# Longer fill at nine stage boundaries, and two products of tile 0 set apart in each stage's first block

## The chip, the cores and the metric

The kernel runs on one core of one Trainium2 chip. The metric is device microseconds of one execution; the time before is the median of three runs, 1781.67 us (1781.33 to 1782.0).

## The reference, cut to what matters

Two transformer blocks of width 1024 run on 256 tokens, each with two layers, so that ten sublayers follow each other. Each is a normalised and modulated input, a body, and a gated residual:

```python
h, g = modulate(x, norm_g[i, 0], c_act, mod_w[i, 0], mod_b[i, 0])   # rmsnorm * (1 + scale) + shift
x = x + 0.5 * g * swiglu(h, ffn_w_gate[i, 0], ffn_w_up[i, 0], ffn_w_down[i, 0])
...
y = mamba2_mixer(...)   # or moba_mixer, stick_breaking_attention, dsa_attention, conv_ffn
x = x + g * y
```

The order of the bodies is ffn, mamba, ffn, ffn, moba, ffn, sb, cffn, dsa, cffn. The weights are fp32, some 280 blocks of 128x2048 elements (1 MB) in all.

## The kernel before

**Stages.** One stage of the program is one sublayer; they are numbered 0 to 9. The activations lie transposed in SBUF: `h` has eight tiles (kk = 0 to 7) of 128 features by 256 tokens. Every fp32 product is made of three fp32r products: both operands are split into a high part and a low remainder, and the kernel adds high x high, high x low and low x high (helper `three`, lines 1573 to 1575). ScalarE makes the high parts of the weights (L495), VectorE their low parts (L913), three buffers in rotation; TensorE works through the blocks in the order in which they lie in memory.

**Tile 0 lies apart.** The low part of `h` is two tensors: tiles 1 to 7 in `h_lo_rest`, tile 0 in `h_lo_first`, with an unused tensor of 16 words before it and one of 48 words behind it:

```python
h_hi = sb("h_hi", [P, KT, T], F32R)
h_lo_rest = sb("h_lo_rest", [P, KT - 1, T], F32R)
gap = sb("gap", [P, 16])
h_lo_first = sb("h_lo_first", [P, T], F32R)
gap2 = sb("gap2", [P, 48])
```

So `h_hi` and `h_lo_rest` begin at the same offset modulo 128 bytes, and `h_lo_first` begins 64 bytes off it. In all later blocks of a stage the products with kk = 0 are written in the order low tile, high tile, low weight (lines 1630 to 1632), once for each half of the output.

**A stage boundary.** The last block of a stage (`last`) ends with the sums of squares for the next norm (`summed_squares`, L1686, or `squares`, L1669). TensorE then runs `fill(st + 1)` (L1695): products whose result goes to a bank that nobody reads before it is overwritten; both operands come from the first weight block of the next stage. Meanwhile ScalarE makes the reciprocal root (L499, L501), VectorE the eight scaled tiles (L1034), ScalarE the eight high tiles `h_hi` (L529, semaphore `hhi`), VectorE the eight low tiles (L1041, semaphore `hlo`) and then the last quarter of the second block's low weights (L920).

**The first block of a stage** (`gemm` with `first=True`) has a high part and a low part. The high part waits for `hhi` of each kk and multiplies it with high and low weights for both halves of the output (L1586, L1589: 32 products). The low part waits for `hlo` of each kk and multiplies it with the high weights, (kk, m) in the order (0,0), (0,1), (1,0), (1,1) to (7,0), (7,1) (L1600: 16 products). In stage 0 the high part is ordered a little differently (low weights in a loop of their own, L1595), the low part is the same, and the second block begins with pairs of low tile (L1606) and high tile (L1608). In stages 1 to 9 what follows is the next block, or the small products of mamba or dsa (`three` with `ws_hi`).

Of the kernel before, what the change touches and what calls it, by code (L numbers as in the profile page):

```python
# [30 lines left out]
KT = D // P  # L31
# [9 lines left out]
MAMBA_SIDE = [None] + [("item", q) for q in (29, 30, 31)] + [("fold", (2, part)) for part in range(4)]  # L41
HELD = range(32, 36)
RESCALED = 6
FILL = {0: 0, RESCALED: 28}
AHEAD = 2
NRAW = 6
NW = 3
# [203 lines left out]
def build(nc, weights, mods, params, consts, xin, out, stages=None):  # L251
# [3 lines left out]
    with ExitStack() as ctx:  # L255
# [16 lines left out]
        def h_lo(kk):  # L272

            return h_lo_rest[:, kk - 1, :] if kk else h_lo_first[:, :]
# [1280 lines left out]
        def _(eng):  # L1555
            k = Steps(eng, plan, sems)

            def begin(st, i, a, b):

                if st == 0 and isinstance(i, int) and i == 0 and b == 0:  # L1560
                    eng.wait_ge(sems["half_lo"], 1)
                elif st == 0 and isinstance(i, int) and i == 0 and b == 1:
                    eng.wait_ge(sems["whi"], k.block(0, b=1) + 1)
                elif st and isinstance(i, int) and i == 0 and b == 1:
                    eng.wait_ge(sems["part"], st)
                else:
                    eng.wait_ge(sems["wlo"], k.block(st, i, a, b) + 1)
                s = k.block(st, 0 if a % NW == 0 else i, a, b) % NW
                return [w[s][:, :] for w in (w_hi, w_lo)]

            def three(dst, ah, al, bh, bl, start, stop, skip=False):

                eng.matmul(dst, ah, bh, start=start, stop=False, skip_group_check=skip)  # L1573
                eng.matmul(dst, ah, bl, start=False, stop=False, skip_group_check=skip)  # L1574
                return eng.matmul(dst, al, bh, start=False, stop=stop, skip_group_check=skip)  # L1575

            def gemm(dst, st, i=0, a=0, b=0, tokens=False, first=False, between=None):

                hi, lo = [w.rearrange("p (k n) -> p k n", k=KT) for w in begin(st, i, a, b)]
                both = [(m, slice(m * P, (m + 1) * P), dst[:, m * T:(m + 1) * T]) for m in range(2)]  # L1580
                if first:

                    for kk in range(KT):
                        k.wait("hhi", st, b=kk)
                        for m, part, d in both:
                            eng.matmul(d, hi[:, kk, part], h_hi[:, kk, :], start=kk == m == 0, stop=False,  # L1586
                                       skip_group_check=True)
                            if st:
                                eng.matmul(d, lo[:, kk, part], h_hi[:, kk, :], start=False, stop=False,  # L1589
                                           skip_group_check=True)  # L1590
                    for kk in range(0 if st else KT):
                        if kk == 4:
                            eng.wait_ge(sems["wlo"], 1)
                        for m, part, d in both:
                            eng.matmul(d, lo[:, kk, part], h_hi[:, kk, :], start=False, stop=False,  # L1595
                                       skip_group_check=True)
                    for kk in range(KT):
                        k.wait("hlo", st, b=kk)
                        for m, part, d in both:
                            mm = eng.matmul(d, hi[:, kk, part], h_lo(kk), start=False, stop=kk == KT - 1,  # L1600
                                            skip_group_check=True)
                elif st == 0 and isinstance(i, int) and i == 0 and b == 1:

                    for kk in range(KT):
                        for m, part, d in both:
                            eng.matmul(d, hi[:, kk, part], h_lo(kk), start=kk == m == 0, stop=False,  # L1606
                                       skip_group_check=True)
                            eng.matmul(d, hi[:, kk, part], h_hi[:, kk, :], start=False, stop=False,  # L1608
                                       skip_group_check=True)
                    eng.wait_ge(sems["wlo"], k.block(0, b=1) + 1)  # L1610
                    for kk in range(KT):
                        for m, part, d in both:
                            mm = eng.matmul(d, lo[:, kk, part], h_hi[:, kk, :], start=False, stop=kk == KT - 1,
                                            skip_group_check=True)
                else:
                    for m, part, d in both:
                        if m and between:
                            between()
                        for kk in range(KT):
                            if m == 0 and kk == 6 and st and isinstance(i, int) and i == 0 and b == 1:  # L1620
                                eng.wait_ge(sems["wlo"], k.block(st, b=1) + 1)
                            if tokens and kk == 0:
                                eng.matmul(d, h_lo(kk)[:, part], hi[:, kk, :], start=True, stop=False)
                                eng.matmul(d, h_hi[:, kk, part], hi[:, kk, :], start=False, stop=False)
                                eng.matmul(d, h_hi[:, kk, part], lo[:, kk, :], start=False, stop=False)
                            elif tokens:
                                mm = three(d, h_hi[:, kk, part], h_lo(kk)[:, part], hi[:, kk, :], lo[:, kk, :],
                                           kk == 0, kk == KT - 1)
                            elif kk == 0:
                                eng.matmul(d, hi[:, kk, part], h_lo(kk), start=True, stop=False)  # L1630
                                eng.matmul(d, hi[:, kk, part], h_hi[:, kk, :], start=False, stop=False)  # L1631
                                eng.matmul(d, lo[:, kk, part], h_hi[:, kk, :], start=False, stop=False)  # L1632
                            else:
                                mm = three(d, hi[:, kk, part], lo[:, kk, part], h_hi[:, kk, :], h_lo(kk),
                                           kk == 0, kk == KT - 1)
                mm.then_inc(sems["blk"], 1)
# [53 lines left out]
            def fill(st):  # L1690


                hi = begin(st, 0, 0, 0)[0].rearrange("p (k n) -> p k n", k=KT)
                for n in range(FILL.get(st, 14)):
                    eng.matmul(bank[5][:, 0:T], hi[:, n % KT, 0:P], hi[:, n % KT, :], start=True, stop=True)  # L1695

            def norm(st):
# [7 lines left out]
            def ffn(st):  # L1705
# [3 lines left out]
                def gate(i, a, b, first=False):  # L1709
                    if not first:  # L1710
                        k.wait(free4, st, i, per4, -per4)
                    gemm(bank[4], st, i, a, b, first=first)

                def up(i, a, b, first=False):
                    if not first:
                        k.wait(free5, st, i, per5, -1)
                    gemm(bank[5], st, i, a, b)
# [29 lines left out]
            def last(st, ready, early=0, token_squares=None):  # L1747
# [37 lines left out]
                if more:  # L1785
                    fill(st + 1)

            def mamba(st):
# [73 lines left out]
                def body(i, a, b):  # L1862
                    more = i > 0
                    k.wait("xdt", st, i, 1, -1)
                    gemm(bank[4], st, i, a, b, first=not more)
                    if more:
                        more_rows(i)
                    else:
                        timestep()
                    k.wait("cbs", st, i, 1, -1)  # L1870
                    gemm(bank[5], st, i, a, b + 1, between=None if more else timestep_columns)
                    if more:
                        y_out(i)
                        k.wait("dec", st, i, 4, -1)
                    gemm(bank[7], st, i, a, b + 2)
                    if not more:
                        cum()
                    parts(i)
                    if more:
                        gemm_out(st, i, a, b + 3, lambda kk: k.wait("alo", st, i, 1, -1) if kk == 0 else None, i == 1)  # L1880
                    first_rows(i)
# [354 lines left out]
```

## Time and profile before

| | |
|---|---|
| median of 3 runs | 1781.67 us |
| profiled execution, its own time | 1790.81 us |
| its span | 1789.0 us |
| granted TensorE clock, mean | 0.999 |
| TensorE busy | 1749.9 us (98%), 14686 matmuls |
| VectorE / ScalarE busy | 1452.8 us (81%) / 956.5 us (53%) |
| chain that ended last | TensorE 90%, VectorE 4%, ScalarE 3%, DMA 2% |

TensorE's ends are modelled and its matmuls overlap: one is listed at some 280 ns, but the next starts some 115 ns later. So the distance from start to start, called the pitch below, is what a matmul costs, and not its listed duration.

### The profile page before, as it was taken

Reading aid. Unit: us, or ns where it says so; the run is one execution under the profiler, and the core shown is the slowest. Engines: PE = TensorE matmul, PEld = TensorE weight load, DVE = VectorE, ACT = ScalarE, POOL = GpSimd, SP = SyncE. Lnnn points to the kernel's source line nnn. Section 1 sums busy time; section 2 is a strip of 40 time slices with the busy share of each in tenths; the row PEclk is TensorE's granted clock in tenths of the full one; section 3 lists DMA queues with packets and bytes.
Section 4 is the critical chain, followed back from the end, with each engine's and each line's share of the span. In section 5 each row is a group of like instructions: output and inputs, shape, how many; then the busy total and the mean of one; then the engine's idle time right before and its main releaser. Section 6 shows DMA issues by size and latency. Waiting matters only on the chain.

```text
span 1789.0 us, 34260 instructions
## 1 busy us (share of the span) xinstructions
PE 1749.9 (98%) x14686; PEld 1700.5 (95%) x14686; DVE 1452.8 (81%) x1749; ACT 956.5 (53%) x1254; POOL 0.2 (0%) x4
## 2 busy tenths in 40 slices
PE   5999999999999999999999999999999999999999
PEld 4999999998999999999999999999999998989999
DVE  7799898888898889898557989765899887567766
ACT  4443466665533354445766444565655556775553
POOL 0000000000000000000000000000000000000000
PEclk9999999999999999999999999999999999999999
DMA  9998834344597949895444989343288545415551
GB/s 396 414 419 307 322 141 154 134 173 154 219 410 312 373 167 386 326 393 193 170 152 186 388 329 378 134 163 139 110 304 292 206 147 177 151 73 214 187 197 37
DMA packets 68149, 426.23 MB, mean 238 GB/s; under 512 B 7488, under 2 KB 10832, under 8 KB 31824
## 3 DMA queue, kind: packets, MB, share of 16 engines
q1 hardware_dynamic: 63936, 416.22, 60.5%
q10 hardware_dynamic: 4112, 8.62, 1.4%
q8 instruction: 68, 1.11, 0.2%
q14 instruction: 33, 0.27, 0.0%
HBM read 423.74 MB, written 3.17 MB: 239 GB/s over the span
## 4 chain that ended last, share of the span: by engine, by line
PE 90%; DVE 4%; ACT 3%; DMA 2%; issue 0%; DVEq 0%; SPq 0%; ACTq 0%
PE bank L1573 24%; PE bank L1574 24%; PE bank L1575 24%; PE bank L1630 2%; PE bank L1632 2%; PE bank L1631 2%; DMA raw<-weights 1%; PE bank L1686 1%; PE bank L1989 1%; DMA mix<-mods 1%; PE bank L1586 1%; PE bank L1600 1%; PE bank L1589 1%; PE bank L1822 1%; ACT w_hi L495 1%; DVE work L1034 1%
## 5 line engine op out<-in xcount | busy, mean ns | idle before, releaser
L1573 PE MATMUL bank<-h_hi,w_hi 128*128 128x256 f32 x2504 | 696.0, 278 | 0.0
L1574 PE MATMUL bank<-h_lo_rest,w_hi 128*128 128x256 f32 x2504 | 694.9, 278 | 0.0
L1575 PE MATMUL bank<-h_hi,w_lo 128*128 128x256 f32 x2504 | 694.8, 277 | 0.0
L913 DVE TENSOR_TENSOR w_lo<-raw,w_hi 128x2048 fp32r<-128x2048 f32 x267 | 609.5, 2284 | 90.4 <-ACT w_hi L495 89.3
L495 ACT ACTIVATE w_hi<-raw 128x2048 fp32r<-128x2048 f32 x276 | 527.9, 1913 | 160.0 <-PE bank L1575 145.7
L1573 PEld LDWEIGHTS bank<-h_hi,w_hi 128*128 128x128 f32 x2504 | 472.8, 189 | 0.0
L1574 PEld LDWEIGHTS bank<-h_lo_rest,w_hi 128*128 128x128 f32 x2504 | 470.2, 188 | 0.0
L1575 PEld LDWEIGHTS bank<-h_hi,w_lo 128*128 128x128 f32 x2504 | 470.1, 188 | 0.0
L1573 PE MATMUL bank<-a_hi,w_hi 128*128 128x256 f32 x1280 | 358.5, 280 | 1.2 <-DVE a_lo L1291 0.8
L1575 PE MATMUL bank<-a_hi,w_lo 128*128 128x256 f32 x1280 | 355.3, 278 | 0.0
L1574 PE MATMUL bank<-a_lo,w_hi 128*128 128x256 f32 x1280 | 355.3, 278 | 0.0
L1573 PEld LDWEIGHTS bank<-a_hi,w_hi 128*128 128x128 f32 x1280 | 241.9, 189 | 3.4 <-issue 1.4
L1574 PEld LDWEIGHTS bank<-a_lo,w_hi 128*128 128x128 f32 x1280 | 240.4, 188 | 0.1
L1575 PEld LDWEIGHTS bank<-a_hi,w_lo 128*128 128x128 f32 x1280 | 240.4, 188 | 0.0
L968 DVE SCALAR_TENSOR_TENSOR macc<-modws,cact,macc 128x1536 f32<-128x1536 f32 x126 | 225.8, 1811 | 1.8 <-DMA modws<-mods 1.8
L1154 DVE SCALAR_TENSOR_TENSOR mix<-bank,par,mix 128x254 f32<-128x254 f32 (+1 forms) x176 | 76.7, 477 | 41.6 <-ACT mix L581 40.0
L1630 PE MATMUL bank<-h_lo_first,w_hi 128*128 128x256 f32 x344 | 100.1, 291 | 1.6 <-DVE work L1376 1.4
L554 ACT ACTIVATE a_hi<-mix 128x512 fp32r<-128x512 f32 x40 | 25.3, 633 | 140.6 <-PE bank L1575 125.3
L1632 PE MATMUL bank<-h_hi,w_lo 128*128 128x256 f32 x344 | 97.9, 285 | 0.0
L1631 PE MATMUL bank<-h_hi,w_hi 128*128 128x256 f32 x344 | 96.6, 281 | 0.0
L581 ACT ACTIVATE mix<-bank,par 128x256 f32<-128x256 f32 x88 | 44.9, 561 | 92.2 <-PE bank L1575 92.2
L540 ACT ACTIVATE mix<-bank 128x512 f32<-128x512 f32 x44 | 26.4, 599 | 116.8 <-PE bank L1575 116.8
(303 smaller groups left out, 1989.4 us busy)
## 6 DMA issues: line engine op xcount, KB each, us to landing
raw<-weights SPq DMA_DIRECT2D x276, 1024.0 KB, 5.4
modws<-mods SPq DMA_DIRECT2D x144, 768.0 KB, 6.6
mix<-mods SPq DMA_DIRECT2D x5, 1024.0 KB, 8.8
mix<-mods ACTq DMA_DIRECT2D x8, 512.0 KB, 13.3
biases<-scratch ACTq DMA_DIRECT2D x1, 2048.0 KB, 13.1
mix<-biases ACTq DMA_DIRECT2D x4, 512.0 KB, 4.0
modws<-mods SPq DMA_DIRECT2D x1, 1024.0 KB, 11.7
x<-xin SPq DMA_DIRECT2D x1, 1024.0 KB, 10.9
```

The source lines that it names most:

```text
L495: eng.activation(w_hi[g % NW][:, :], raw[g % NRAW][:, :], ACT.Copy).then_inc(sems["whi"], 1)
L540: k.inc("silu", eng.activation(sg, bank[4][:, :].rearrange("p (a t) -> p a t", a=2), ACT.Silu))
L581: ins = eng.activation(dst[:, m, :], b[:, m * T:(m + 1) * T], ACT.Identity, scale=cw(i, t, 2), bias=cw(i, t, 3))
L913: eng.tensor_tensor(w_lo[g % NW][:, :], raw[g % NRAW][:, :], w_hi[g % NW][:, :], ALU.subtract).then_inc(sems["wlo"], 1)
L968: ins = eng.scalar_tensor_tensor(out=m, in0=modw[q % 4], scalar=c, in1=m, op0=ALU.mult, op1=ALU.add)
L1154: ins = eng.scalar_tensor_tensor(out=dst[:, m, lag:T], in0=b[:, m * T:(m + 1) * T - lag], scalar=cw(i, 22 * up + m, tap), in1=dst[:, m, la ...
L1573: eng.matmul(dst, ah, bh, start=start, stop=False, skip_group_check=skip)
L1574: eng.matmul(dst, ah, bl, start=False, stop=False, skip_group_check=skip)
L1575: return eng.matmul(dst, al, bh, start=False, stop=stop, skip_group_check=skip)
L1630: eng.matmul(d, hi[:, kk, part], h_lo(kk), start=True, stop=False)
L1631: eng.matmul(d, hi[:, kk, part], h_hi[:, kk, :], start=False, stop=False)
L1632: eng.matmul(d, lo[:, kk, part], h_hi[:, kk, :], start=False, stop=False)
```

## The change

Three edits, all in TensorE's program. The fill becomes 20 products where it was 14, and 36 where it was 28 (the boundary to stage 6, which has a second norm; stage 0 has none). In the low part of each stage's first block, stage 0 too, the product (0,1) leaves its place behind (0,0) and goes between (7,0) and (7,1); every wait stays where it was.

```diff
-FILL = {0: 0, RESCALED: 28}
+FILL = {0: 0, RESCALED: 36}
...
                     for kk in range(KT):
                         k.wait("hlo", st, b=kk)
-                        for m, part, d in both:
-                            mm = eng.matmul(d, hi[:, kk, part], h_lo(kk), start=False, stop=kk == KT - 1,
+                        turns = ((0, 0),) if kk == 0 else ((7, 0), (0, 1), (7, 1)) if kk == 7 else ((kk, 0), (kk, 1))
+                        for n, m in turns:
+                            _, part, d = both[m]
+                            mm = eng.matmul(d, hi[:, n, part], h_lo(n), start=False, stop=n == KT - 1,
                                             skip_group_check=True)
...
-                for n in range(FILL.get(st, 14)):
+                for n in range(FILL.get(st, 20)):
                     eng.matmul(bank[5][:, 0:T], hi[:, n % KT, 0:P], hi[:, n % KT, :], start=True, stop=True)
```

## Rows read from the trace of the kernel before

**Rows 1.** Windows, TensorE alone: stretch, busy (matmuls), granted clock, DMA share, GB/s

```profile
500.00:620.00 120.00, 120.00 (x1021) 1.00 0.92 363
680.00:800.00 120.00, 120.00 (x1054) 1.00 0.94 369
...
80.00:200.00 120.00, 120.00 (x1022) 1.00 0.95 376
```

**Rows 2.** Windows, TensorE alone: whole stages 2 and 3, fill to fill

```profile
458.76:650.13 191.37, 190.87 (x1612) 1.00 0.83 329
650.13:836.25 186.12, 185.61 (x1613) 1.00 0.83 322
```

**Rows 3.** Timeline of TensorE, boundary to stage 3: start, duration, line, count

```profile
650.13 2.02 PE L1695 MATMUL bank<-w_hi 128*128 128x256 f32 x14
652.65 0.36 PE L1586 MATMUL bank<-h_hi,w_hi 128*128 128x256 f32 x1 [0.50 <-ACT h_hi L529]
652.84 0.28 PE L1589 MATMUL bank<-h_hi,w_lo 128*128 128x256 f32 x1
```

**Rows 4.** Chain that ended last, boundary to stage 3: start, us, what

```profile
652.00 0.52 ACT h_hi L529
652.51 0.14 issue
```

**Rows 5.** Timeline of TensorE, boundary to stage 6

```profile
1142.49 3.71 PE L1695 MATMUL bank<-w_hi 128*128 128x256 f32 x28
1146.92 0.36 PE L1586 MATMUL bank<-h_hi,w_hi 128*128 128x256 f32 x1 [0.72 <-ACT h_hi L529]
```

**Rows 6.** Timeline of TensorE, stage 3, end of high part, low part, next block

```profile
656.38 0.28 PE L1589 MATMUL bank<-h_hi,w_lo 128*128 128x256 f32 x1
656.50 0.40 PE L1600 MATMUL bank<-h_lo_first,w_hi 128*128 128x256 f32 x2
656.73 1.77 PE L1600 MATMUL bank<-h_lo_rest,w_hi 128*128 128x256 f32 x14
658.33 0.28 PE L1630 MATMUL bank<-h_lo_first,w_hi 128*128 128x256 f32 x1
658.45 0.28 PE L1631 MATMUL bank<-h_hi,w_hi 128*128 128x256 f32 x1
...
658.93 0.28 PE L1575 MATMUL bank<-h_hi,w_lo 128*128 128x256 f32 x1
```

**Rows 7.** Timeline of TensorE, stage 2: first product, end of high part, low part

```profile
461.28 0.36 PE L1586 MATMUL bank<-h_hi,w_hi 128*128 128x256 f32 x1 [0.49 <-ACT h_hi L529]
...
464.89 0.28 PE L1589 MATMUL bank<-h_hi,w_lo 128*128 128x256 f32 x1
465.01 0.39 PE L1600 MATMUL bank<-h_lo_first,w_hi 128*128 128x256 f32 x2
465.24 1.85 PE L1600 MATMUL bank<-h_lo_rest,w_hi 128*128 128x256 f32 x14
466.93 0.28 PE L1630 MATMUL bank<-h_lo_first,w_hi 128*128 128x256 f32 x1
```

**Rows 8.** Timeline of TensorE, stage 0, end of first block and second block

```profile
38.81 1.11 PE L1600 MATMUL bank<-h_lo_rest,w_hi 128*128 128x256 f32 x8
39.75 0.28 PE L1606 MATMUL bank<-h_lo_first,w_hi 128*128 128x256 f32 x1
...
39.99 0.28 PE L1606 MATMUL bank<-h_lo_first,w_hi 128*128 128x256 f32 x1
...
41.15 0.28 PE L1606 MATMUL bank<-h_lo_rest,w_hi 128*128 128x256 f32 x1
...
43.30 0.28 PE L1608 MATMUL bank<-h_hi,w_hi 128*128 128x256 f32 x1
```

**Rows 9.** Timeline of VectorE, boundary to stage 3

```profile
655.05 2.85 DVE L1041 SCALAR_TENSOR_TENSOR h_lo_rest<-work,modv,h_hi 128x256 fp32r<-128x256 f32 x7
657.83 0.68 DVE L920 TENSOR_TENSOR w_lo<-raw,w_hi 128x512 fp32r<-128x512 f32 x1
```

## The prediction

> **What bounds the kernel now.** The page comes first: TensorE is busy 98% of the span and makes up 90% of the chain that ended last, with the three lines of `three` at 24% each. VectorE (81%) and ScalarE (53%) are behind it. So only three things can move the time: the number of matmuls outside idle stretches, TensorE's idle time, and the pitch. The list of TensorE's waits says how little idle there is at the nine boundaries: about half a microsecond each before the first L1586, 0.72 us at stage 6 [rows 3, 5]. All of it together is some 5 us, and it is time in which the norm is made by ScalarE and VectorE, so no filler can win it back.
>
> The third view, the windows of TensorE alone, shows the pitch, and here is the surprise. In 120 us of stage 2 there are 1021 matmuls, in 120 us of stage 3 there are 1054, at the same granted clock (1.00, the 2.4 GHz level) and nearly the same DMA share [rows 1]. That is a pitch of 120 / 1021 = 0.1175 us against 120 / 1054 = 0.1139 us. Both numbers hold the few slower products at each tile change; in the plain stretches I read 0.118 and 0.113. Stages 2 and 3 are the same program on other weights (1612 and 1613 matmuls), and stage 2 takes 191.37 us against 186.12 us [rows 2]. So there are two paces, a slow and a fast one, and a stage keeps the one with which it leaves its first blocks. Stage 0 is slow between 80 and 200 us [rows 1]; it got there by a wait at 72 us that this change doesn't touch. The long plain stages after a boundary are 2, 3, 5, 7 and 9; of these only stage 2 is slow now.
>
> Where is the pace set? In stage 3 the high part runs slow: 31 steps from 652.65 to 656.38, 0.120 each [rows 3, 6]. Then two products of `h_lo_first` follow each other, and after them the pace is fast: 14 steps in 1.60 us from 656.73 to 658.33, 0.114 each [rows 6]. In stage 2 it is the other way round: high part 3.61 us for 31 steps (0.116, the first step after the idle time included), low part 1.69 us for 14 steps (0.121) [rows 7]. I went through all nine boundaries: 1, 2, 6 and 8 go as stage 2, from fast to slow; 3, 4, 5, 7 and 9 as stage 3, from slow to fast. Two products of tile 0 one behind the other turn the pace over, each time. A single product of tile 0, as at every later tile change, doesn't: in stage 3 it costs some slower steps (658.33 to 658.93 is 0.60 us for five steps where 0.57 is plain) and the fast pace returns [rows 6]; in stage 2 the slow pace returns.
>
> One place more bears on the change. In stage 0 the low part ends slow (38.81 to 39.75, 8 steps, 0.1175), then come tile 0, high tile, tile 0, high tile (39.75, 39.99), and by 41.15 the pace is fast: 19 steps in 2.15 us to 43.30, 0.113 each [rows 8]. So tile 0, other, tile 0, other turns slow into fast as well.
>
> **The change part by part.**
>
> *Fill.* It adds 8 x 6 + 8 = 56 matmuls. At stage 3 the 14 take 2.02 us with the tail of the last; their pitch is 0.120 once they run. The last one starts at 650.13 + 2.02 - 0.28 = 651.87, and six more put the next slot at 651.87 + 7 x 0.12 = 652.71. The first L1586 starts at 652.65 but is listed at 0.36 us instead of 0.28, and the second follows after 0.19 instead of 0.12, so it really begins to stream near 652.73 [rows 3]. The added six end where the wait ends. At stage 6, last start 1142.49 + 3.71 - 0.28 = 1145.92, plus 9 x 0.12 gives 1147.00, and 1146.92 + 0.08 is the same [rows 5]. Cost: nothing, since ScalarE's first high tile (652.00 to 652.51, then 0.14 us) is what releases TensorE [rows 4]; if that cover were gone, 56 x 0.12 = 6.7 us. Bounds: 0 to 0.06 us a boundary; I take 0.02, together 0.2 us.
>
> Whether the first product gains is a question of its own: could its weights load under the last filler and save 0.08 us? The trace puts the wait ahead of the weight load, so I take no gain; bound -0.7 us for nine. The Trainium skill (TensorE: Matmul & The Clock Gate, section Step-by-step: what each phase is for) says the queue pulls weight loads ahead of running matmuls, which could give those 0.08 us; no row before shows it across a wait.
>
> *Order, end of the low part.* Between the wait for the eighth `hlo` and the next block there are now three products instead of two. At stage 3 VectorE's last low tile ends at 655.05 + 2.85 = 657.90 [rows 9]; (7,0) started at 658.33 - 2 x 0.113 = 658.10, so not held by it. It now stands one place earlier, at 657.99 to 658.03, and can't start before about 657.90 + 0.14 (the release time of [rows 4]) = 658.04; three steps later it is 658.38 to 658.39, against 658.33. That is +0.06 us. Where (7,0) already waited for its tile (boundaries 1, 2, 6, 8, whose low part began earlier relative to VectorE) it is a whole product, +0.12. Sum 5 x 0.06 + 4 x 0.12 = 0.8 us. The weights of the second block that L920 ends (658.51) are needed only later and were not waited for [rows 9].
>
> *Order, pace.* Tile 0 now comes singly at (0,0), so the pace of the high part should last through the low part. Then come (7,0), tile 0, (7,1), and in ffn and cffn stages the next block begins with tile 0 (L1630): tile 0, other, tile 0, other, the sequence of stage 0. If the pace at (7,0) is slow, it leaves fast. What will the high part's pace be? Every boundary's first steps after the idle time are slow (0.116 to 0.118), and four of nine turned fast within five steps [rows 7]. The filler's operands both lie at the offset of tile 0, and its steady pitch is 0.120, the step seen between the two tile-0 products that end in the slow pace. A fill that runs into the high part without a pause should therefore start it slow, the same way each time. I take slow at all nine.
>
> *Sum.* Stage 2 becomes as stage 3: 186.12 - 191.37 = -5.25 us [rows 2]; by the counts of [rows 1] it would be 1612 x (0.1175 - 0.1139) = -5.8. Stages 1, 6 and 8 are slow for only 20 to 60 products after their first block now, at 0.0045 us each, -0.3 together at most (mamba and dsa don't go on with L1630; I take -0.2). Stages 3, 5, 7, 9 and 4 stay fast, 0. Stage 0 has a third tile 0 close behind; its pace between 45 and 73 us could turn slow, some 245 x 0.0045 = +1.1, or not; I take 0.2. Sum: 0.2 + 0.8 - 5.25 - 0.2 + 0.2 = -4.25 us. Against the profiled execution: 1790.81 - 4.25 = 1786.6. That execution is 9.1 us above the median of the runs; I take the difference over unchanged, although whether stage 2 is slow in unprofiled runs too no view can say. 1781.67 - 4.25 = 1777.4.
>
> **The rivals.**
>
> *No turn: the pace isn't moved (0.24).* Either the slow pace of stage 2 stays, or it belongs to the profiled execution alone. Then what is left is the third product behind the last tile and the seam: +0.2 + 0.8 = +1.0, 1782.7; 1781 with 0.08 us won at each seam. For it: the sequence that should help was seen once, with high tiles between [rows 8]. Against: two-in-a-row turned the pace at nine of nine boundaries. [...]
>
> *The wrong turn (0.28), slower.* The high part is fast after the joined fill, as it became at four of nine boundaries, and the close pair at the end turns fast into slow, as two in a row did there. Then stages 3, 5, 7, 9, now fast, become slow at +5.25 us each. It decides from the first: stage 2 slow still and one more is 1781.67 + 1.0 + 5.25 = 1787.9; all four, 1803.7. With stage 2 won and one of the others lost it is even, 1782.7. For it: nothing shows what tile 0, other, tile 0 does to the fast pace. Against: stages 3, 4, 5, 7 and 9 had slow high parts after a pause, and a fill at 0.120 looks like the slow side.
>
> *The fill overruns (0.03).* If a fill product cost more, every boundary slips: at 0.13 the slot is 0.07 later, nine times 0.6 us: 1778.0, or 1783.3 without the turn. Inside the cases above.
>
> **How the numbers follow.** Forecast 0.45, no turn 0.24, wrong turn 0.28, overrun 0.03 (split between the first two). A measurement of this kernel tells about 0.2%, 3.6 us, from no change. The forecast lies at -4.25 with stage 0 and the seams as its spread: 1775.5 to 1778.5, its own range. Nearly all of it is faster, a little falls within 0.2%; the no-turn case is the same, as is the even mix of a stage won and a stage lost; of the wrong turn most is slower. So faster 0.46, same 0.28, slower 0.26. The range runs from 1775 to 1788: it holds the forecast, no turn, and the wrong turn at one stage; it leaves out two or more stages lost (about 0.15) and more than one gain (0.03).
>
> **What would show it.** In the windows of the changed kernel, stage 2 with some 1054 matmuls in 120 us and about 186 us long; stages 3, 5, 7, 9 unchanged. At the boundaries: no idle time before L1586 (or below 0.05 us), L1695 at 20 and 36, the first L1586 within 0.05 us of its place behind the fill's start, the high part at 0.118 in all nine, the low part at 0.118 too, and 0.113 from the next block on. The wait at (7,0) shows as one longer step there. I am wrong if a stage of 3, 5, 7, 9 shows 1021 in 120 us, if stage 2 still does, or if the high parts are fast.

## The result, and the profile after

The changed kernel has a median of 1785.38 us over ten runs (1782.07 to 1795.13), the kernel before 1781.67 us (1780.94 to 1786.84). The ratio is 1.0023, with a 95% interval of 1.0012 to 1.0034: a little slower, where I had forecast 0.2% faster. The median is inside the range that I gave and the sign is not the one forecast.

More telling than the medians are the single runs, in us:

```
before : 1780.94 1781.04 1781.33 1781.39 1781.67 1781.67 1782.00 1782.64 1782.67 | 1786.84
changed: 1782.07 1782.07 1782.42 1783.32 1783.48 | 1787.29 1787.33 1788.36 1788.90 | 1795.13
```

They fall into groups some 5 us apart. Two things have happened: the lowest group moved up by 0.75 us (median 1782.42 against 1781.67), and half of the runs left it. The profiled execution of the kernel before (1790.81 us), on which I had built everything, lies in none of the groups of these ten runs of before.

The windows of TensorE in the changed kernel (stretch, busy, matmuls in brackets, granted clock, DMA share, GB/s) answer to [rows 1] and [rows 2]:

```profile
500.00:620.00 120.00, 120.00 (x1021) 1.00 0.91 362
680.00:800.00 120.00, 120.00 (x1055) 1.00 0.93 367
80.00:200.00 120.00, 120.00 (x1054) 1.00 0.96 384
454.46:645.96 191.50, 191.49 (x1617) 1.00 0.83 329
645.96:832.34 186.38, 186.36 (x1617) 1.00 0.83 321
```

Stage 2 is as slow as before, 1021 matmuls in 120 us and 191.50 us long. Stages 3, 5, 7 and 9 are still fast. Stage 0, which this change touches only in its first block, went from 1022 to 1054 in 120 us. Its slow pace had cost the profiled execution of before 4.4 us, an estimate from these counts: some 1240 products behind the wait at 72 us, at 120/1022 - 120/1054 = 0.0036 us each.

The boundary to stage 3, on the timeline of TensorE, against [rows 3] and [rows 6]:

```profile
646.24 2.74 PE L1697 MATMUL bank<-w_hi 128*128 128x256 f32 x20
648.82 0.30 PE L1586 MATMUL bank<-h_hi,w_hi 128*128 128x256 f32 x1
648.96 0.28 PE L1589 MATMUL bank<-h_hi,w_lo 128*128 128x256 f32 x1
...
652.47 0.28 PE L1602 MATMUL bank<-h_lo_first,w_hi 128*128 128x256 f32 x1
652.59 1.86 PE L1602 MATMUL bank<-h_lo_rest,w_hi 128*128 128x256 f32 x13
654.29 0.28 PE L1602 MATMUL bank<-h_lo_first,w_hi 128*128 128x256 f32 x1
654.41 0.29 PE L1602 MATMUL bank<-h_lo_rest,w_hi 128*128 128x256 f32 x1
654.53 0.28 PE L1632 MATMUL bank<-h_lo_first,w_hi 128*128 128x256 f32 x1
```

The fill ends where the wait ended: there is no idle time in front of the first L1586. Nor are the 0.08 us won that the prediction asked about: the second product of the high part starts 648.96 - 646.24 = 2.72 us after the fill, before 652.84 - 650.13 = 2.71 us [rows 3]. The high part now runs fast from its start (648.82 to 652.47, 32 steps of 0.114), so the low part begins earlier and catches up with VectorE. VectorE's timeline says where its last low tile ends:

```profile
651.15 2.86 DVE L1041 SCALAR_TENSOR_TENSOR h_lo_rest<-work,modv,h_hi 128x256 fp32r<-128x256 f32 x7
```

651.15 + 2.86 = 654.01, and the next block starts at 654.53, 0.52 us later. Before, it was 658.33 - 657.90 = 0.43 us [rows 6, 9]. That is the third product behind the last tile: 0.09 us here, where the prediction had 0.06. At all nine boundaries of this trace the distance is 0.51 to 0.52 us. Before it was 0.39 to 0.40 at the four whose last product had waited, and 0.42 to 0.44 at the five others.

### The profile page after: what moved, and what is told of

The parts are those of the page before. It is cut to its first block, busy times and chain, and to the rows that moved or that the text cites. A ratio compares the mean times of both kernels' runs of the same rounds, so it can differ in the third digit from the quotient of the medians.

```text
span 1787.1 us, 34372 instructions
## 1 busy us (share of the span) xinstructions
PE 1752.9 (98%) x14742; PEld 1704.7 (95%) x14742; DVE 1452.6 (81%) x1749; ACT 956.5 (54%) x1254; POOL 0.2 (0%) x4
## 4 chain that ended last, share of the span: by engine, by line
PE 94%; DVE 2%; ACT 2%; DMA 1%; issue 0%; DVEq 0%; SPq 0%; ACTq 0%
PE bank L1573 25%; PE bank L1574 24%; PE bank L1575 24%; PE bank L1632 2%; PE bank L1634 2%; PE bank L1633 2%; PE bank L1697 1%; PE bank L1688 1%; PE bank L1586 1%; PE bank L1602 1%; PE bank L1991 1%; DMA mix<-mods 1%; PE bank L1589 1%; PE bank L1824 1%; ACT w_hi L495 1%; PE bank L1859 1%
```

## The experiments

All kernels of one session ran on one chip with the kernel before beside them. Slow stages are seen in a trace only; for the other runs they are read from the time, some 5 us for each. How often the kernel before leaves its lowest group differs from chip to chip, so each is read against its own neighbour:

| kernel | runs | below 1786 us, their median | 1786 to 1790.5 | above 1790.5 |
|---|---|---|---|---|
| before, first chip | 29 | 25, 1782.11 | 4 | 0 |
| fill alone | 12 | 6, 1782.46 | 6 | 0 |
| order alone | 12 | 5, 1783.61 | 5 | 2 |
| whole change again | 12 | 6, 1782.57 | 3 | 3 |
| tile 0 aligned | 5 | 0 | 0 | 5 (1815.93 to 1817.70) |
| before, second chip | 31 | 14, 1782.37 | 15 | 2 |
| (0,1) at tile 3 | 12 | 4, 1781.92 | 7 | 1 |
| fill of 17 | 12 | 5, 1782.80 | 5 | 2 |
| fill of 22 | 12 | 12, 1783.68 | 0 | 0 |
| paired | 8 | 8, 1778.28 | 0 | 0 |
| before, third chip | 11 | 4 (1782.22 to 1782.64, and 1785.85) | 6 | 1 |

The limit of 1786 us cuts cleanly except at two places: the 1785.85 us on the third chip belongs with the group above, and of the five runs of the order alone two lie between the groups, at 1784.86 and 1785.65 us.

### The fill alone

```diff
-FILL = {0: 0, RESCALED: 28}
+FILL = {0: 0, RESCALED: 36}
...
-                for n in range(FILL.get(st, 14)):
+                for n in range(FILL.get(st, 20)):
```

> The fill of 20 and 36 alone, the order of the low part as before. Theory A (what the result suggests): the pace of a long stage is drawn anew in each execution, the profiled execution of before had two slow stages (0 and 2, 9.5 us) and nearly all its other runs none; the fixed cost of the change is the third product behind the last low tile, and the rest of the slowdown are stages that fall into the slow pace. Then this kernel's fastest runs are within 0.5 us of the fastest of before (1781), no 0.9 us above, and runs 4.4 to 5.3 us above the fastest are as rare as before if the order is what makes them, or as common as in the changed kernel (half) if the fill is. Rival B: the added fillers themselves cost 0.1 us a boundary; then the fastest runs are at 1782 or above.

Median 1785.43, ratio 1.0013 (1.0002 to 1.0023). The lowest run is 1781.84, and the lowest group sits 0.35 us above that of before: the 56 products cost little. But 6 of 12 runs are in the next group, against 4 of 29 beside them (by chance alone a difference like this would be seen in about 4 cases of 100). In its trace seven of nine high parts are fast, where [rows 7] stands for four of nine. Stage 3 from fill to fill takes 186.10 us with the longer fill, 186.12 before [rows 2]:

```profile
641.15:827.25 186.10, 186.09 (x1618) 1.00 0.83 322
```

### The order alone

```diff
-                        for m, part, d in both:
-                            mm = eng.matmul(d, hi[:, kk, part], h_lo(kk), start=False, stop=kk == KT - 1,
+                        turns = ((0, 0),) if kk == 0 else ((7, 0), (0, 1), (7, 1)) if kk == 7 else ((kk, 0), (kk, 1))
```

> The order of the low part alone, fill of 14 and 28. Theory A: the fastest runs stand 0.7 to 1.0 us above the fastest of before (0.06 to 0.12 us at each of ten low parts), and the next block starts 0.52 us after the last low tile instead of 0.39 to 0.43. If the order makes the slow stages, several of the runs lie 4 to 10 us higher; if the fill does, none or one. Rival B: the fastest runs equal those of before.

Median 1787.92, ratio 1.0027 (1.0013 to 1.0041). Lowest run 1783.26; the five runs below 1786 us have a median 1.5 us above before, the lowest three of them 1.2: more than the 0.7 to 1.0 expected, and more than the whole change, which holds the same order (0.46). No run says why. 7 of 12 runs are above 1786 us. The trace was taken in a run of 1788.55 us, and its slow stage is 2 again.

### The whole change once more

> The changed kernel once more, with a second trace. Theory A: its fastest runs at 1782 to 1782.5, other runs 4 to 13 us above, and the second trace has its slow stages elsewhere than the first, whose only slow long stage is 2. If the pace were fixed by the program, the same stage would be slow again and the runs would agree within 1 us.

Median 1785.91, ratio 1.0025 (1.0008 to 1.0042). This run's trace (1783.34 us) has no slow long stage. Windows of TensorE, to be laid beside those of the changed kernel above, which is the same program:

```profile
500.00:620.00 120.00, 120.00 (x1054) 1.00 0.93 371
680.00:800.00 120.00, 120.00 (x1055) 1.00 0.94 369
80.00:200.00 120.00, 120.00 (x1054) 1.00 0.96 384
```

So the pace of a stage isn't fixed by the program: it differs between executions, and this is worth 5 us a long stage. That it isn't only the chip either is seen in the times, since the twelve runs on this one chip fall into the same groups (1782.2 to 1783.7, 1788.1 to 1789.0, 1793.0 to 1794.6). Both takings of the changed kernel together have 11 of 22 runs above 1786 us, the runs of before beside them 5 of 39; that is no chance (about 2 in 1000).

### Tile 0 at the offset of the others

```diff
-        gap = sb("gap", [P, 16])
+        gap = sb("gap", [P, 32])
...
-        gap2 = sb("gap2", [P, 48])
+        gap2 = sb("gap2", [P, 32])
```

> Before, with the unused tensor ahead of h_lo_first at 32 words instead of 16 and the one behind it at 32 instead of 48: tile 0 then begins at the same offset modulo 128 bytes as the other tiles, nothing else moves. If the offset of tile 0 is what disturbs and turns the pace, the slower steps at each tile change (119, 118, 124, 118 ns) go, some 26 ns at each of about 340 places or 9 us less where a stage is fast, but a pace once slow stays slow through a stage and through the low part. If the offset doesn't matter, the time and the steps are those of before.

Median 1816.85, ratio 1.019 (1.0177 to 1.0204), all five runs within 2 us. The windows of TensorE in stages 0, 2, 3, 5, 7 and 9:

```profile
80.00:200.00 120.00, 120.00 (x1021) 1.00 0.94 372
500.00:620.00 120.00, 120.00 (x1021) 1.00 0.92 363
680.00:800.00 120.00, 120.00 (x1021) 1.00 0.92 355
985.00:1105.00 120.00, 120.00 (x1021) 1.00 0.91 355
1310.00:1430.00 120.00, 120.00 (x1021) 1.00 0.76 271
1660.00:1780.00 120.00, 120.00 (x1022) 1.00 0.48 172
```

Every long stage is slow. Four of its nine high parts still ran fast, and all four fell into the slow pace at the start of the low part; none of the stages stayed fast. A read address moved by 64 bytes, with no product more or less, is worth 35 us. The expected gain of 9 us could not show, since no stage stayed fast.

The trace says more closely what the 64 bytes do. Stage 3 turned fast here too, and lost it at the next tile change:

```profile
661.53 0.28 PE L1575 MATMUL bank<-h_hi,w_lo 128*128 128x256 f32 x1
...
663.69 0.28 PE L1630 MATMUL bank<-h_lo_first,w_hi 128*128 128x256 f32 x1
...
664.86 0.28 PE L1574 MATMUL bank<-h_lo_rest,w_hi 128*128 128x256 f32 x1
```

That is 19 steps of 0.114 us ahead of it and 10 steps of 0.117 behind. Away from waits this trace has 24 tile changes met in the fast pace, and all 24 left it slow; in the trace of before, with tile 0 off by 64 bytes, 215 of 216 stayed fast. At the start of the low part the four fast high parts turned slow without the offset as well, and the five slow ones stayed slow. So the turn from fast to slow at this place needs no offset of tile 0; what is seen only with the 64 bytes is that slow turns fast there, and that a fast pace outlives a tile change.

### (0,1) at tile 3 instead of tile 7

```diff
-... else ((7, 0), (0, 1), (7, 1)) if kk == 7 else ...
+... else ((3, 0), (0, 1), (3, 1)) if kk == 3 else ...
```

> Fill of 14 and 28; in the low part the product (0,1) stands between (3,0) and (3,1), so tile 0 is still met singly, but only two products follow the wait for the last low tile, as before. Against the order of the change with the same fill (fastest runs 1783.3, 7 of 12 runs above 1787): Theory A, the third product behind the last tile costs 0.9 us in all runs: the fastest come back to 1781 to 1782. If meeting tile 0 singly is what leaves stages slow, still about half of the runs lie 5 us or more higher; if the place at the end is (tile 0 just behind the wait, and again just after), slow runs become as rare as before (4 of 29).

Median 1787.35, ratio 1.0009 (0.9994 to 1.0025). The lowest group is at 1781.92, 0.45 us below that of before on this chip: with two products behind the last tile the fixed cost is gone (in the trace 0.39 to 0.47 us from the last low tile to the next block). On the pace this says nothing, since on this chip the kernel before itself had 17 of 31 runs above 1786 us, and 8 of 12 is not different from that.

### A fill of 17

```diff
-FILL = {0: 0, RESCALED: 28}
+FILL = {0: 0, RESCALED: 32}
...
-                for n in range(FILL.get(st, 14)):
+                for n in range(FILL.get(st, 17)):
```

> Order of before, fill of 17 and 32, which leaves 0.25 us of idle time before the high part. If joining the fill to the high part without a pause is what raises the share of slow runs from 4 of 29 to 6 of 12, this kernel is as before: one or two slow runs of 12, fastest at 1781 to 1782. If every added filler raises it, it lies between. If the 6 of 12 was chance, the same as before too, and the next kernel as well.

Median 1787.29, ratio 1.0012 (0.9997 to 1.0027), 7 of 12 runs above 1786 us. Inconclusive for the same reason. The idle time left before the high part is 0.13 to 0.15 us in the trace (0.24 at stage 6).

### A fill of 22

```diff
-FILL = {0: 0, RESCALED: 28}
+FILL = {0: 0, RESCALED: 38}
...
-                for n in range(FILL.get(st, 14)):
+                for n in range(FILL.get(st, 22)):
```

> Order of before, fill of 22 and 38: the high part starts 0.23 us later than its tile would let it, and the low part doesn't catch up with the last low tile. Theory C, the wait in the low part is a rescue (high part fast, two tile-0 products turn it slow, the wait lets it change again): without the wait such stages stay slow for sure, and most runs have two to four slow long stages, 1792 to 1802. Theory D, the wait is what spoils the pace: no slow stages at all, all runs within 1 us at 1782 to 1783 (0.1 us more a boundary).

Median 1783.68, all twelve runs between 1782.72 and 1784.50, none above, while the kernel before beside it had 17 of 31. The ratio is 0.9991 (0.9978 to 1.0003). Timeline of TensorE at the boundary to stage 3:

```profile
641.96 2.98 PE L1695 MATMUL bank<-w_hi 128*128 128x256 f32 x22
644.78 0.29 PE L1586 MATMUL bank<-h_hi,w_hi 128*128 128x256 f32 x1
...
648.42 0.39 PE L1600 MATMUL bank<-h_lo_first,w_hi 128*128 128x256 f32 x2
648.66 1.81 PE L1600 MATMUL bank<-h_lo_rest,w_hi 128*128 128x256 f32 x14
650.30 0.28 PE L1630 MATMUL bank<-h_lo_first,w_hi 128*128 128x256 f32 x1
...
651.24 0.28 PE L1575 MATMUL bank<-h_hi,w_lo 128*128 128x256 f32 x1
...
652.38 0.28 PE L1573 MATMUL bank<-h_hi,w_hi 128*128 128x256 f32 x1
```

Here nothing waits: 14 steps of the low part take 650.30 - 648.66 = 1.64 us (0.117, slow), and after the next block's single tile 0 the pace turns fast (651.24 to 652.38, ten steps of 0.114). All nine boundaries of this trace have a fast high part and a slow low part, and every long stage is fast. That is Theory D's outcome and not my Theory C's, with a spread of 1.8 us where 1 was expected: where TensorE meets no wait between the fill and the next block, the outcome was the same at nine boundaries of one trace and, by the times, in twelve runs. It costs 1.3 us in the lowest group, since the high part starts 0.23 us after its tile would let it.

These nine turns from slow to fast came at a single tile 0, against the prediction's "a single product of tile 0 ... doesn't". The trace of before has such a turn too, at stage 6, with the same order of products that left stage 2 slow [rows 7]:

```profile
1150.87 1.86 PE L1600 MATMUL bank<-h_lo_rest,w_hi 128*128 128x256 f32 x14
1152.57 0.28 PE L1630 MATMUL bank<-h_lo_first,w_hi 128*128 128x256 f32 x1
...
1153.04 0.28 PE L1574 MATMUL bank<-h_lo_rest,w_hi 128*128 128x256 f32 x1
...
1153.49 0.28 PE L1575 MATMUL bank<-h_hi,w_lo 128*128 128x256 f32 x1
```

The low part takes 0.121 a step with its one wait, and from 1153.04 on four steps take 0.45 us, 0.113 each.

### Tile 0 of both halves drawn together

```diff
+                elif not tokens and not between:
+                    for m, part, d in both:
+                        eng.matmul(d, hi[:, 0, part], h_lo(0), start=m == 0, stop=False, skip_group_check=True)
+                        eng.matmul(d, hi[:, 0, part], h_hi[:, 0, :], start=False, stop=False, skip_group_check=True)
+                    for m, part, d in both:
+                        eng.matmul(d, lo[:, 0, part], h_hi[:, 0, :], start=False, stop=False, skip_group_check=True)
+                    for m, part, d in both:
+                        for kk in range(1, KT):
...
+                            mm = three(d, hi[:, kk, part], lo[:, kk, part], h_hi[:, kk, :], h_lo(kk),
+                                       False, kk == KT - 1, True)
```

> Before, with the tile-0 products of both halves of a block drawn together in the plain blocks of all ffn and cffn stages and all others that take this path: low tile, high tile, low tile, high tile, then both low weights, then tiles 1 to 7 of each half. The same products, in another order. If tile 0, other, tile 0 heals a slow stage and leaves a fast one fast, no run has a slow stage and the spread shrinks to 1 us; and with one disturbance a block instead of two, some 26 ns at 170 places or 4 us less in the fast runs: 1777 to 1778. If the pair turns either pace over at every block, half of all blocks are slow: 1790 to 1800 in every run.

Median 1778.28, all eight runs between 1777.36 and 1778.91; ratio 0.9967 (0.9955 to 0.998). Windows of TensorE in stages 2, 3 and 0, and the head of one block on the timeline:

```profile
500.00:620.00 120.00, 120.00 (x1058) 1.00 0.93 373
680.00:800.00 120.00, 120.00 (x1058) 1.00 0.94 373
80.00:200.00 120.00, 120.00 (x1057) 1.00 0.97 385
```

```profile
501.04 0.28 PE L1617 MATMUL bank<-h_lo_first,w_hi 128*128 128x256 f32 x1
501.16 0.28 PE L1618 MATMUL bank<-h_hi,w_hi 128*128 128x256 f32 x1
501.28 0.28 PE L1617 MATMUL bank<-h_lo_first,w_hi 128*128 128x256 f32 x1
501.39 0.28 PE L1618 MATMUL bank<-h_hi,w_hi 128*128 128x256 f32 x1
501.52 0.39 PE L1620 MATMUL bank<-h_hi,w_lo 128*128 128x256 f32 x2
501.75 0.28 PE L1573 MATMUL bank<-h_hi,w_hi 128*128 128x256 f32 x1
```

1058 instead of 1054 in 120 us: one disturbance a block instead of two, 4 us over the kernel. And by the times no run has a slow long stage. A fast pace is left fast: 616 of 616 pairs in later blocks, away from waits, in the five traces of paired kernels. A slow one mostly turns fast, 19 of 24, and at the other five the next pair did it. So the pair restores the fast pace within a few blocks, which is what the prediction read from stage 0 [rows 8], though not at each pair.

### The change on top of the paired kernel

With slow stages out of the way, small costs can be measured. The same edits as above, on the paired kernel, on a third chip (before beside them: 11 runs, 7 above 1786 us and one at 1785.85):

> The whole change (fill of 20 and 36, order of the low part) on top of the paired tile-0 products of the later blocks, which kept every run free of slow stages (1777.4 to 1778.9). With slow stages out of the way the times show the fixed cost alone. Theory A: about 1.0 us above the paired kernel without the change on the same chip, all of it the third product behind the last low tile (0.12 us at boundaries where TensorE waits for it, 0.09 else), and no run 4 us or more above the others. Rival: slow stages come back, since the change spoils the pace in a way that the pair doesn't heal.

> The longer fill alone on top of the paired kernel. Theory A: the added 56 products lie in TensorE's wait for the first high tile and cost nothing: within 0.3 us of the paired kernel. Rival B: each seam costs 0.03 to 0.1 us, 0.3 to 0.9 us in all.

> The order of the low part alone on top of the paired kernel, fill of 14 and 28. Theory A: 0.8 to 1.1 us above the paired kernel, as much as the whole change. Rival B: no more than the fill alone.

> The paired kernel once more, on the chip of the three others, as their reference: 1777.4 to 1778.9 as before, no slow stage, some 4 us below the fastest runs of the kernel before.

| on the paired kernel | median us | runs | ratio to before |
|---|---|---|---|
| nothing | 1778.31 | 1777.99 to 1779.19 | 0.996 (0.9946 to 0.9973) |
| fill of 20 and 36 | 1778.15 | 1777.54 to 1778.49 | 0.9959 (0.9945 to 0.9972) |
| order | 1779.45 | 1778.63 to 1780.15 | 0.9968 (0.9956 to 0.98) |
| both | 1779.96 | 1779.16 to 1780.61 | 0.9966 (0.9954 to 0.9979) |

The fill costs nothing (-0.16 us), the order 1.14 us, both 1.65 us. These are differences of medians of five or six runs that spread over 1 to 1.5 us, so half a microsecond more or less is not told apart. By the times no run has a slow long stage. Best of all kernels that I ran is the paired one, with or without the longer fill: 4.1 us below the lowest group of before on both of its chips.

Part of what the order costs lies behind the boundary. Stages 2 and 5 from fill to fill, first with the whole change, then with the fill alone:

```profile
454.87:641.08 186.21, 186.19 (x1618) 1.00 0.85 338
943.79:1133.47 189.68, 189.36 (x1632) 1.00 0.80 316
453.82:639.58 185.76, 185.75 (x1618) 1.00 0.85 339
941.93:1131.15 189.22, 188.90 (x1632) 1.00 0.81 316
```

Each is some 0.45 us longer with the order, of which the third product is 0.09 to 0.12. The rest fits the first blocks, which ran slow until their third pair turned them.

## Why the prediction was wrong

**The failing step is "a stage keeps the one with which it leaves its first blocks ... of these only stage 2 is slow now".** I took the paces of one execution for those of the kernel. That execution, 9.1 us above the median, had two slow stages, 0 and 2, worth 4.4 and 5.25 us. Nine of the ten runs of before beside the change lie at 1780.94 to 1782.67; none of them was traced, but the traces of the fill alone (1781.84 us) and of (0,1) at tile 3 (1781.92 us) have no slow long stage. So the term -5.25 us could not be earned: in nine of ten runs there was nothing to win. And where stage 2 was slow, the change didn't mend it: in its own trace stage 2 is slow from end to end. The text had the hint and let it pass, "whether stage 2 is slow in unprofiled runs too no view can say", and then took the difference over unchanged. 9.1 us is near enough to 4.4 + 5.25 that it should have been the first reading.

**"I take slow at all nine" was wrong as well.** With the fill joined on, seven of nine high parts are fast in the traces of the changed kernel and of the fill alone, four of nine in the second trace of the change. Over all traces 29 of 45 high parts are fast behind the fill of 20, 25 of 63 behind that of 14; such a difference comes by chance in about 2 cases of 100, so the fill seems to shift the pace towards fast, against the reason that I gave, the filler's pitch of 0.120. A fast high part reaches the low tiles sooner and waits for the last one or two.

**"If the pace at (7,0) is slow, it leaves fast" came true about as often as not.** The five traces with the new order have 35 boundaries behind which a block begins with tile 0. Of the 18 with a slow high part 10 were fast from about the tenth product of that block on, of the 17 with a fast high part 5.

**The end of the low part.** The sum had +0.8 us for the third product and +0.2 us for the seams, 1.0 together. On the kernel itself the lowest group moved by 0.75 us and, the second time, by 0.46. Measured on the paired kernel: order 1.14, fill nothing, both 1.65. The mechanism was right and is seen on the timeline (0.52 us from last tile to next block); the size agrees within what these runs can tell. Two things point to more than the sum had: five boundaries were counted at half a product where 0.08 to 0.09 us were lost, and a stage that leaves the wait slow stays so for one or more blocks, which the sum had at nothing and which is seen in stages 2 and 5 of the paired kernel.

**Tile 0 and the pace.** Two tile-0 products in a row turned the pace over in 63 of 63 boundaries of the seven traces with the old order and the offset kept; that reading holds. (The 0.120 and 0.121 that the prediction read for the slow parts hold one long step each, 0.19 at the first product and some 0.16 at the last tile; the plain steps are 0.118.) The one that a single tile 0 doesn't turn it does not: nine of nine single visits behind a boundary turned slow into fast in the trace of the fill of 22. Tile 0, other, tile 0, other restored the fast pace in the paired kernel, if not at each pair; in the changed kernel, whose pair stands right behind a wait and comes once a stage, it often didn't. That the wait is to blame, and not that it comes only once, no run shows.

**The rivals.** The case that came closest is "no turn", with its second reason, the slow pace that belongs to the profiled execution alone: it gave 1782.7, and the lowest group of the changed kernel is at 1782.4. What it lacked is the other half: the change makes slow stages likelier, from 5 of 39 runs to 11 of 22, one or two stages at a time, at the 5.25 us each of the "wrong turn". Its condition, fast high parts, was met; its outcome was not four lost stages but, by the times, none, one or two. The overrun didn't happen. That the median, 1785.38, fell within the range is luck: it lies between two groups, in a gap where no run is.

**What stays open.** Why a given wait ends in one pace or the other, and why the kernel before draws slow stages in 1 of 10, 4 of 29, 17 of 31 and 8 of 11 runs in four sessions. On the last two of these chips the change might have looked like no change; by itself it was not run there. Whether the fill or the order does more harm to the pace can't be told either: 6 and 7 of 12.

## What to carry to other kernels

When a profiled execution stands well above the median of the runs, find out first what in it is not in the others, before a step rests on it; several times of one kernel, sorted, show it for nothing. Count matmuls per window: a stream that never waits can still run at two paces, and then what matters is not to save products but to make the pace the same each time, by keeping waits out of the boundary (the fill of 22) or by a sequence that restores it often (the paired kernel). A product moved behind the last thing that is waited for costs its whole pitch.

## What the runs showed of the hardware

TensorE has two pitches for the same stream of 128x128 by 128x256 fp32r products at the same granted clock, 1.00: 0.113 and 0.118 us. It can stay in one for a whole stage of 191 us. The address of the moving operand modulo 128 bytes bears on it: alike for all tiles, every long stage was slow (1021 products in 120 us, 1816.85 us); one tile in eight off by 64 bytes, stages can be fast (1054), and with the visits to that tile in pairs there are 1058. A visit costs 26.7 ns in the fast pace and nothing in the slow one (means over 215 and 87 visits in the trace of before, worked out from the steps).

The pace changes at such visits and at waits, and not the same way in each execution. The waits at the end of a low part are short: steps of 0.14 to 0.23 us in place of 0.113 or 0.118. In stage 0 of before a wait of 0.36 us at 72.53 turned fast into slow with no tile 0 near it. Why a wait ends in one pace or the other is open, and so is what in TensorE's reads makes the 64 bytes count.
